# Expert weights of a mixture-of-experts encoder block on one Trainium2 core: loads of two chunks at a time in place of one

## The reference

```python
h = rmsnorm(x)
qA,kA,vA,qB,kB,vB,gate_A,gate_B = split(h @ w_in)
oa = global attention of 8 query heads over 2 kv heads (axial rotary)
ob = attention within 128 tokens of 8 query heads over 2 kv heads (with a sink logit)
x = x + (sigmoid(gate_A) * (oa @ w_branch_a) + sigmoid(gate_B) * (ob @ w_branch_b)) @ w_out
h2 = rmsnorm(x)
# 4 of 32 experts for each token, softmax over the chosen logits
gu = h2 @ w_gate_up[e] + b_gate_up[e]               # 1024 -> 2048
y  = clamped_swiglu(gu) @ w_down[e] + b_down[e]     # 1024 -> 1024
x = x + sum over the chosen experts of gate * y
return rmsnorm(x)
```

## Time and profile before

| | |
|---|---|
| three executions | 1508.18, 1508.53, 1511.29 us; median 1508.53 |
| the profiled execution | 1511.68 us, span 1509.9 us |
| granted TensorE clock, mean | 0.992 |
| busy share of the span | TensorE 99%, VectorE 87%, ScalarE 76%, GpSimd 25% |
| moved by DMA | 457 MB, mean 303 GB/s |
| chunk loads | 384 of 1024 KB |

### The profile page before, as it was taken

One profiled execution on the slowest core, in us unless ns is written; L12 is line 12 of the kernel. 1 busy time (PEld: TensorE's weight loads), 2 busy tenths in 40 slices (PEclk: granted clock), 3 DMA queues, 4 the chain that ended last, 5 costly groups with the idle time before them and its releaser, 6 DMA issues.

```text
span 1509.9 us, 21672 instructions
## 1 busy us (share of the span) xinstructions
PE 1491.5 (99%) x7202; PEld 1229.6 (81%) x7204; DVE 1307.4 (87%) x1029; ACT 1152.2 (76%) x1262; POOL 385.0 (25%) x214
## 2 busy tenths in 40 slices
PE   8999999998999999999999999999999999999998
PEld 6888789887788888888888888888888888888885
DVE  5477587655999999999999999999999999999986
ACT  6355588234888888888888888888888888888883
POOL 1002245401243221323123221222321233222110
PEclk9999999998999999999999999999999999999999
DMA  7330001634999999999999999999999999999973
GB/s 259 113 112 28 1 1 57 212 140 177 371 378 371 386 382 376 383 377 380 379 379 372 384 379 374 382 376 376 380 378 373 376 382 377 384 379 382 382 279 133
DMA packets 130659, 457.17 MB, mean 303 GB/s; under 512 B 13987, under 2 KB 14507, under 8 KB 130629
## 3 DMA queue, kind: packets, MB, share of 16 engines
q1 hardware_dynamic: 118852, 435.19, 75.8%
q0 software_dynamic: 9360, 16.51, 4.3%
q10 hardware_dynamic: 2416, 5.07, 0.9%
HBM read 451.77 MB, written 22.54 MB: 314 GB/s over the span
## 4 chain that ended last, share of the span: by engine, by line
PE 96%; DVE 2%; ACT 1%; DMA 0%; issue 0%; DVEq 0%; SPq 0%; ACTq 0%
PE ps L1609 28%; PE ps L1611 28%; PE ps L1610 28%; PE ps L1898 2%; PE ps L1906 2%; PE ps L1667 1%; PE ps L1710 1%; PE ps L1711 1%; PE ps L1840 1%; PE ps L2046 1%; PE ps L1652 0%; DMA raw<-in_w_in 0%; ACT probs L815 0%; PE ps L1684 0%; PE ps L1685 0%; PE ps L1688 0%
## 5 line engine op out<-in xcount | busy, mean ns | idle before, releaser
L1418 DVE TENSOR_TENSOR chunk_lo<-chunk,chunk_hi 128x2048 fp32r<-128x2048 f32 x384 | 889.3, 2361 | 31.2 <-ACT chunk_hi L929 29.2
L929 ACT ACTIVATE chunk_hi<-chunk 128x2048 fp32r<-128x2048 f32 x378 | 719.5, 1913 | 72.5 <-PE ps L1611 72.5
L1609 PE MATMUL ps<-chunk_hi,XT 128*128 128x512 f32 x1024 | 404.5, 395 | 0.3 <-DVE XT L1458 0.3
L1611 PE MATMUL ps<-chunk_hi,XT 128*128 128x512 f32 x1024 | 399.1, 390 | 0.0
L1610 PE MATMUL ps<-chunk_lo,XT 128*128 128x512 f32 x1024 | 398.9, 390 | 0.0
L1611 PEld LDWEIGHTS ps<-chunk_hi,XT 128*128 128x128 f32 x1024 | 192.2, 188 | 40.4
L1609 PEld LDWEIGHTS ps<-chunk_hi,XT 128*128 128x128 f32 x1024 | 192.4, 188 | 39.1 <-DVE XT L1458 0.8
L1610 PEld LDWEIGHTS ps<-chunk_lo,XT 128*128 128x128 f32 x1024 | 192.5, 188 | 38.0
L678 POOL DMA_INDIRECT sum_rows<-y,idx x31 | 74.5, 2404 | 493.2 <-ACT y L1079 493.2
L1609 PE MATMUL ps<-chunk_hi,hidT 128*128 128x512 f32 x512 | 199.3, 389 | 0.0
L1611 PE MATMUL ps<-chunk_hi,hidT 128*128 128x512 f32 x512 | 199.2, 389 | 0.0
(11 more groups left out here) (293 smaller groups left out, 1998.5 us busy)
## 6 DMA issues: line engine op xcount, KB each, us to landing
chunk<-in_w_gate_up SPq DMA_DIRECT2D x256, 1024.0 KB, 11.7
chunk<-in_w_down SPq DMA_DIRECT2D x128, 1024.0 KB, 10.3
raw<-in_w_in SPq DMA_DIRECT2D x14, 1024.0 KB, 5.4
xs<-in_x SPq DMA_DIRECT2D x8, 512.0 KB, 6.4
w_out<-in_w_out SPq DMA_DIRECT2D x4, 1024.0 KB, 6.0
raw<-in_w_branch_a SPq DMA_DIRECT2D x2, 1024.0 KB, 5.5
raw<-in_w_branch_b SPq DMA_DIRECT2D x2, 1024.0 KB, 6.4
sum_rows<-xs ACTq DMA_DIRECT2D x4, 512.0 KB, 2.7
```

Of the source, the lines that this page charges most:

```text
L929: a.activation(chunk_hi[hi_slot(c, nxt)][:, :], chunk[c][:, :], ACT.Copy).then_inc(ex_hi, 1)
L1418: v.tensor_tensor(chunk_lo[c][:, :], chunk[c][:, :], chunk_hi[hi_slot(c, nxt, first)][:, :].bitcast(F32), ALU.subtract).then_inc(ex_lo, 1)
L1609: mm(dst, lhsT(0), rhs(0), start=start, stop=False, skip_group_check=seeded)
L1611: return mm(dst, lhsT(1), rhs(0), start=False, stop=stop, skip_group_check=seeded)
```

## The change

Two neighbouring chunks become one transfer of 2 MB with one semaphore. The places in SBUF stay: chunks 2p and 2p+1 lie next to each other already, and `chunk_two` and `lo_two` name both together. A pair is asked for when the second of its chunks has been used. Chunk 0's first load moves from half of `merged` to all of it, because chunk 1's place is free only then; the bias rows of expert 0 are now issued behind it. The splits and matmuls stay 1 MB pieces in the same order, and both halves wait for the pair's semaphore.

```diff
-        chunk = [at(f"chunk{c}", CH_AT[c], [128, SLOT]) for c in range(NCH)]
-        chunk_lo = [at(f"chunk_lo{c}", CH_AT[c], [128, SLOT], F32R) for c in range(NCH)]
+        chunk_two = [at(f"chunk_two{c}", CH_AT[c], [128, 2 * SLOT]) for c in range(0, NCH, 2)]
+        lo_two = [at(f"chunk_lo_two{c}", CH_AT[c], [128, 2 * SLOT], F32R) for c in range(0, NCH, 2)]
+        chunk = [chunk_two[c // 2][:, c % 2 * SLOT:(c % 2 + 1) * SLOT] for c in range(NCH)]
+        chunk_lo = [lo_two[c // 2][:, c % 2 * SLOT:(c % 2 + 1) * SLOT] for c in range(NCH)]
...
-        expert_in = [sem(f"expert_in{s}") for s in range(NCH)]
+        expert_two = [sem(f"expert_in{s}") for s in range(NCH // 2)]
+        expert_in = [expert_two[s // 2] for s in range(NCH)]
...
-                w = w_gate_up[0, e, q * 256:(q + 1) * 256, (c // 4) * FF:(c // 4 + 1) * FF]
+                w = w_gate_up[0, e, q * 256:(q + 2) * 256, (c // 4) * FF:(c // 4 + 1) * FF]
             else:
-                w = w_down[0, e, q * 256:(q + 1) * 256, :]
-            return w.rearrange("(k p) n -> p k n", k=2)
+                w = w_down[0, e, q * 256:(q + 2) * 256, :]
+            return w.rearrange("(k p) n -> p k n", k=4)
...
-            sp.dma_start(chunk[c][:, :].rearrange("p (k n) -> p k n", k=2), expert_src(e, c)).then_inc(expert_in[c], 16)
+            sp.dma_start(chunk_two[c // 2][:, :].rearrange("p (k n) -> p k n", k=4), expert_src(e, c)).then_inc(expert_two[c // 2], 16)
...
+            sp.wait_ge(merged, KD)
             load_expert(sp, 0, 0)
-            sp.wait_ge(merged, KD)
             sp.dma_start(bias_first[32:33, :], b_gate_up[0, 0:1, 0:FF]).then_inc(row_g_in, 16)
             sp.dma_start(bias_first[64:65, :], b_gate_up[0, 0:1, FF:2 * FF]).then_inc(row_u_in, 16)
-            load_expert(sp, 1, 0)
             sp.wait_ge(branch_ps, KD)
             load_expert(sp, 2, 0)
-            load_expert(sp, 3, 0)
...
-            for c in range(4):
-                sp.wait_ge(ex_used, c + 3)
+            for c in range(0, 4, 2):
+                sp.wait_ge(ex_used, c + 4)
                 load_expert(sp, c, 1)
...
             with sp.Fori(1, last_item) as i:
-                for c in range(4):
-                    sp.wait_ge(ex_used, 12 * i + c - 1)
+                for c in range(0, 4, 2):
+                    sp.wait_ge(ex_used, 12 * i + c)
                     load_expert(sp, c, (i + 1) % E)
-                for c in range(8, 12):
-                    sp.wait_ge(ex_used, 12 * i + c - 5)
+                for c in range(8, 12, 2):
+                    sp.wait_ge(ex_used, 12 * i + c - 4)
                     load_expert(sp, c, i % E)
                 load_rows(sp, i + 2, (i + 2) % E)
-                for c in range(4, 8):
-                    sp.wait_ge(ex_used, 12 * i + c + 3)
+                for c in range(4, 8, 2):
+                    sp.wait_ge(ex_used, 12 * i + c + 4)
                     load_expert(sp, c, (i + 1) % E)
-            for c in range(8, 12):
-                sp.wait_ge(ex_used, 12 * last_item + c - 5)
+            for c in range(8, 12, 2):
+                sp.wait_ge(ex_used, 12 * last_item + c - 4)
                 load_expert(sp, c, last_item % E)
```

4 lines of the change are left out of this document (2 added, 2 removed).

## The result

The changed kernel takes 1519.74 us (median of 4 runs, 1518.69 to 1522.95), the kernel before on the same chip 1509.51: a ratio of 1.0067, 95% interval 1.0053 to 1.0081. It is slower by 10.2 us, outside the predicted range. The profiled execution took 1519.2 us with a span of 1517.4, 7.5 us over the span of before; what follows accounts for these 7.5.

The account below looks back on a forecast made before the run. TensorE was taken to bound the loop, with the transfers a second, nearly equal bound. Terms of 0 (loop), 0.2 (first item) and 0.5 (last item) sum to 0.7 us on a median of 1508.53: 1509.2 us, range 1506 to 1517.

Parts of the forecast that it names:

- The two bounds: Expert loop: TensorE's period and the DMA engines' work are both 34.6 us an item, equal within what can be read.
- Common landing and the slack of the loop: Loop: pair lands when its second chunk did; 1.5 us slack plus 2.8 us lead covers 4.3 us; cost 0.
- Rival A: Loop: transfers become the bound, 0.6 us an item lost after 7 items, 14 us, so 1523; chance 0.12.
- The first item: Expert 1's first loads: chunk 0 waits 1.3 us for its pair; TensorE loses 0 to 0.9 us, taken as 0.2.
- A pair into an empty queue: Load queue: a pair with little ahead of it lands in 4.9 + 2.54 = 7.4 us.
- The last item: Chunks 8 to 11 at the end: last pair 0.3 us late, scatter may delay it; 0.5 us, bounds 0 and 3.2.
- rival C: Last item: all 4.1 us of scatter and gather ahead of the pair, bound of 3.2 us, 1512.6; chance 0.06.
- Fewer issues and the first loads: SyncE's six dma_start for twelve an item, and chunk 0's later first load at the kernel's head: 0 each.
- 2 MB against 1 MB: Transfer efficiency in the loop: same 4 KB rows and bytes, fixed part already hidden; taken as 0.
- Rival B: Loop: pairs push hidT 0.3 us behind its need in each item, 9 us over 31 items: 1518; chance 0.06.
- D: Routing and end: idle there could shrink, 1 us guessed, 1507.5; chance 0.04 for more than 3 us faster.
- E: Whole kernel: nothing changes, every cover holds, 1508.5; chance 0.72 together with the main forecast and D's mild side.

Follow-up runs that it names:

- light_before: Kernel before with one of three matmuls (hi by lo) left out of every expert product: 1507.00 us, ratio 0.9976.
- heavy2_before: Kernel before with two more hi by lo matmuls in each item: 1524.64 us, ratio 1.0105.
- late_issue: Against the kernel before: single 1 MB loads, a semaphore each, issued two together at the changed kernel's moments: 1536.03 us, ratio 1.0173.
- heavy2_late_issue: late_issue with two more hi by lo matmuls in each item: 1544.24 us, ratio 1.0236 to the kernel before.
- after_again: The changed kernel once more, unaltered, beside the kernel before: 1519.84 us, ratio 1.0056.
- light_after: Changed kernel with one of three matmuls (hi by lo) left out of every expert product: 1501.91 us, ratio 0.9947 to the kernel before.
- late_and_common: Kernel before with 1 MB loads issued two together at the pairs' moments and ScalarE waiting for both: 1555.82 us, ratio 1.0305.
- first_rows_early: Changed kernel with the first item's half of XT ahead of chunk 2's split on ScalarE and VectorE: 1520.15 us, ratio 1.0065.
- heavy6_after: Changed kernel with six more hi by lo matmuls in each item: 1557.59 us, ratio 1.0329 to the kernel before.
- loop_single: Changed kernel with pairs only ahead of the loop and in the first item, single 1 MB loads in the loop: 1514.58 us, ratio 1.0031.
- head_single: Changed kernel with all loads ahead of the loop single 1 MB as before, pairs from then on: 1519.03 us, ratio 1.0063.

## Why the prediction was wrong, by its steps

**The two bounds.** "The two are equal within what I can read" was right as far as it goes. The growth built on it was misread. 0.57 us an item is chunk 4's alone (7.8 to 14.7 us); chunk 5 goes from 11.3 to 14.5 between the same items, and the mean of all loads from 8.4 to 12.4 over 600 us, or 17.3 items: 0.23 an item. From 1055 us on it stays between 12.3 and 12.7, at 34.6 us an item and without a loss. In the changed kernel the mean starts at 11.5, grows by 0.28 an item and comes to 17.5 at 1268 us. Nor does an item give the DMA engines one fixed amount of work, 34.6 us: with everything waiting for loads it took 35.04 (light_before), and at 35.05 the landings of heavy2_before are level while those of late_issue's loads grow (heavy2_late_issue).

**Common landing and the slack of the loop.** Predicted: the pair lands when its second chunk landed before, with 1.5 us of slack and 4.3 us with the leads behind it, cost 0. This step failed, and the loop lost 3.3 us in the profiled execution and 11.7 in after_again's. The pair (6, 7), which the prediction has landing at 1250.8, lands at 1257.4, of which 3.0 is the kernel's general delay and 3.6 its own lateness; ScalarE waits 0.25 us for it. The 4.3 us weren't used up in that place. Two things were missing. First, a pair is asked for later and still takes about 3 us more on average from the start of the loop (11.5 against 8.6 for the second chunks before). The window of 400 to 420 us has the DMA engines at a share of 0.92 for 1.00 before; that this idle time is the cause is argued, not shown. Second, landings grow by another 5 us by 1268 us. The prediction's slack was read in one item and held for all. And the lead that broke was another, the 2.0 us of `y` before TensorE's lookup, which the prediction never looked at.

**Rival A** named the mechanism that came true: the transfers become the bound, the margin is used up item by item, and then every item loses. It had the growth of 0.57 us an item in its hands and worked out "3 us, so 1512" from going on with it; that is the size of the profiled loop's loss (3.3), but by luck: at 0.23 an item the 13 items behind 1055 us give 3 us, less than the margin of 4.3. It got 0.12 because it was tied to a price of pairs in the queue, and no run shows such a price: in light_after and late_and_common the 2 MB transfer is the cheaper one. The chance should have hung on the distance to the edge, not on the cost of the transfer. Once an execution has begun to lose, an item takes 34.9 to 36.1 us (after and after_again), so that an early start costs 10 us and more (11.7 in after_again).

The Trainium skill (DMA: Bandwidth & Descriptors, Specifications) has about 358 GB/s as one core's limit from HBM, by which, as an estimate, an item's chunks take 35.1 us. The runs moved 376 to 381 GB/s over 960 us, gather and scatter included, so this core wasn't held to that figure, and the prediction was right to set it aside. That the 12.6 MB of chunks in the 35.04 us of light_before come to 359 GB/s bears on nothing else that was measured here. The conclusion that it set aside with the figure, that loads bind in both versions, was nearer to the truth than its own all the same.

**The first item**, 0.2 predicted with bounds 0 and 0.9: 2.7 measured, the step that failed most plainly. ScalarE's wait was right (1.65 for 1.3). The cover was read from the wrong consumer: `hid` has a lead of 1.1, but the half of `XT`, which stands directly behind the late split, has 0.12. first_rows_early moved it and got 1.35 of the 2.7 back in that item.

**A pair into an empty queue**: 7.4 assumed as 4.9 + 2.54. Measured: at least 7.5 for the pair (8, 9) of the last item, 7.7 in heavy6_after and light_after, and 7.7 to 8.0 for the very first pair in seven executions, so the assumption was 0.3 to 0.6 short. The Trainium skill's fit (DMA: Bandwidth & Descriptors, Anatomy of one DMA), which is for transfers issued by GpSimd, gives an estimate of 6.8 for 2 MB and 4.4 for 1 MB; these loads of SyncE took 7.7 to 8.0 and 4.8 to 5.0.

**The last item**, 0.5 with bounds 0 and 3.2: 1.2 measured. The mechanism was right and the term mis-sized: (10, 11) takes 9.1 us, of which scatter and gather are some 1.5 us (the estimate above), more than the 0.5 allowed and less than rival C's 4.1.

**Fewer issues and the first loads**, 0 each: the head of the kernel differs by 0.5 us, inside its own spread. **2 MB against 1 MB**, 0: if anything a small gain (35.04 to 34.70 us an item in the light kernels' profiled executions), and none that shows at TensorE's 34.6. **Rival B**, a steady wait: heavy6_after, with the same orders and common landings, loses nothing in the loop, and the changed kernel keeps 34.6 us for 24 items. It fell, as did **D** (faster) and **E** (every cover holds). Of the signs that the prediction named for being wrong, landings of 19 us came, and ScalarE's waits for loads in every item, these from 968 us on; fewer GB/s in the loop didn't (378 for 379).

The sum by the runs is 0.5 - 0.2 + 2.7 + 3.3 + 1.2 = 7.5 us for the profiled execution. The medians' 10.2 is for the most part the same, taken from a before that is 2.2 us faster than its profiled execution. How it is shared out may differ between executions, as after_again's 11.7 in the loop shows.

## What to carry to other kernels

Where two bounds are within a per cent of each other, read the growth of the time from issue to landing over the whole loop, not the engine's busy share and not one item, and ask in which item the growth meets the reserve: a change that only asks later moves that item forward. To price a late input, take the lead of each thing that stands behind it in the same engine's order, and use the smallest. To test which of two near-equal bounds holds, make one of them a little slower or much faster in both versions, and see whether their difference goes. And where a load counts as landed with its last increment, look at the one before it too: a mean busy share says nothing about one part that lags.

## What the hardware showed that was not expected

- One transfer of 2 MB was better than two of 1 MB asked for at the same moment, by 36 us in 1556 with common landings (late_and_common against after_again), yet 2 MB into an empty queue landed in 7.7 to 8.0 us where 1 MB took 4.8 to 5.0.
- The growth of the landings was in the last of the 16 increments alone: 12.5 us where the fifteenth came at 7.9 in the kernel before, 16.8 and 10.6 in the changed one.
- The same loads need a different time an item by the state of the queue: late_issue's take about what light_before's do, 34.8 to 35.0 us, when all waits for them (1507.02 and 1507.00 us in all), and 35.9 when TensorE asks for 35.05.
- One program on one chip spread from 1509.8 to 1523.4 us (loop_single) and from 1513.0 to 1529.7 (head_single), as against 1507.2 to 1514.3 in 90 of 91 runs of the kernel before, and 1517.1 in one.
- Leaving out a third of TensorE's expert matmuls brought the granted clock in the loop from 1.00 to 0.90 and the time down by only 3 us, with the loop itself 8 us longer.
